# Two turns of a transformer kernel run by token halves

## The reference

```python
h = _rmsnorm(hres, norm_g[i, 0])
m = _diff_attention(...) if i % 2 == 0 else _short_conv(h, w_in[i], conv_w[i // 2], w_out[i])
hres = hres + _rmsnorm(m, norm_g[i, 1])
h = _rmsnorm(hres, norm_g[i, 2])
hres = hres + _rmsnorm(_sqrelu_mlp(h, w_up[i], w_down[i]), norm_g[i, 3])
```

## Time and profile before

| | us |
|---|---|
| median of 3 runs | 1973.28 (1971.84 to 1976.45) |
| the profiled execution's own time | 1971.16 |
| its span, first to last instruction | 1969.4 |
| PE busy | 1887.1 (96%) |
| DVE busy | 1387.8 (70%) |
| ACT busy | 839.2 (43%) |
| POOL busy | 149.8 (8%) |

### The profile page before, as it was taken

How to read it: one execution, slowest core, us unless ns; L and a number is a source line. 1 busy time by engine, 2 the same in 40 slices (tenths; PEclk the granted TensorE clock), 3 DMA queues, 4 the chain that set the end, 5 groups by cost and what they waited for, 6 DMA issues and landing times.

```text
span 1969.4 us, 30367 instructions
## 1 busy us (share of the span) xinstructions
PE 1887.1 (96%) x12322; PEld 1699.5 (86%) x12322; DVE 1387.8 (70%) x2110; ACT 839.2 (43%) x1286; POOL 149.8 (8%) x126
## 2 busy tenths in 40 slices
PE   7999889999999899999998999999899989999996
PEld 6876777899999788989898999999899868988995
DVE  8676738788786866666649877776655469777764
ACT  4555434444443444444435444443422245444441
POOL 3000021000000320000012000000300130000001
PEclk9999999999999999999999999999899989999998
DMA  5220121232333221111111322222122212323221
GB/s 182 67 105 22 54 86 65 86 108 86 108 108 107 86 86 65 44 44 44 65 65 65 108 96 98 89 105 108 45 87 105 86 66 106 107 86 107 107 86 43
DMA packets 26085, 166.54 MB, mean 85 GB/s; under 512 B 3808, under 2 KB 4064, under 8 KB 6624
## 3 DMA queue, kind: packets, MB, share of 16 engines
q1 hardware_dynamic: 25232, 163.52, 23.6%
q10 hardware_dynamic: 720, 1.14, 0.2%
HBM read 162.55 MB, written 2.10 MB: 84 GB/s over the span
## 4 chain that ended last, share of the span: by engine, by line
PE 46%; DVE 4%; ACT 1%; issue 0%; ACTq 0%
PE ps L2857 6%; PE ps L2858 6%; PE ps L2859 6%; PE ps L2873 4%; PE ps L2872 4%; PE ps L2871 4%; PE ps L402 4%; PE ps L404 4%; PE ps L403 4%; DVE ps L560 1%; DVE h L577 1%; DVE z_lo L511 1%; PE ps L2644 0%; PE ps L2646 0%; PE ps L2645 0%; PE ps L449 0%
## 5 line engine op out<-in xcount | busy, mean ns | idle before, releaser
L402 PE MATMUL ps<-z_hi,w_hi 128*128 128x512 f32 (+1 forms) x736 | 259.8, 353 | 31.3 <-DVE z_lo L511 28.0
L384 DVE TENSOR_TENSOR w_lo<-w_raw,w_hi 128x2048 fp32r<-128x2048 f32 x93 | 214.0, 2301 | 64.6 <-ACT w_hi L373 64.5
L403 PE MATMUL ps<-z_lo,w_hi 128*128 128x512 f32 (+1 forms) x736 | 255.3, 347 | 0.0
L404 PE MATMUL ps<-z_hi,w_lo 128*128 128x512 f32 (+1 forms) x736 | 254.8, 346 | 0.0
L2857 PE MATMUL ps<-arena,w_hi 128*128 128x256 f32 (+2 forms) x768 | 245.5, 320 | 0.5 <-DVE acc L2134 0.5
L2858 PE MATMUL ps<-arena,w_hi 128*128 128x256 f32 (+2 forms) x768 | 245.9, 320 | 0.0
L2859 PE MATMUL ps<-arena,w_lo 128*128 128x256 f32 (+2 forms) x768 | 245.4, 320 | 0.0
L373 ACT ACTIVATE w_hi<-w_raw 128x2048 fp32r<-128x2048 f32 x93 | 177.1, 1905 | 71.8 <-PE ps L404 59.0
L402 PEld LDWEIGHTS ps<-z_hi,w_hi 128*128 128x128 f32 x736 | 142.9, 194 | 56.7 <-issue 22.7
L404 PEld LDWEIGHTS ps<-z_hi,w_lo 128*128 128x128 f32 x736 | 142.5, 194 | 17.5
L403 PEld LDWEIGHTS ps<-z_lo,w_hi 128*128 128x128 f32 x736 | 143.1, 194 | 16.8 <-issue 0.7
(11 more groups left out here) (415 smaller groups left out, 5081.8 us busy)
## 6 DMA issues: line engine op xcount, KB each, us to landing
w_raw<-wstream SPq DMA_DIRECT2D x151, 1024.0 KB, 4.8
out<-h SPq DMA_DIRECT2D x8, 256.0 KB, 2.0
w_raw<-wstream SPq DMA_DIRECT2D x2, 512.0 KB, 6.2
h<-xT ACTq DMA_DIRECT2D x4, 256.0 KB, 6.6
h<-xT SPq DMA_DIRECT2D x4, 256.0 KB, 6.1
rope_cs<-pT SPq DMA_DIRECT2D x1, 512.0 KB, 5.5
acc<-pos SPq DMA_DIRECT2D x1, 256.0 KB, 10.5
acc<-lam SPq DMA_DIRECT2D x1, 128.0 KB, 9.9
```

What stands on the lines that cost most here:

```text
L384: dve.tensor_tensor(w_lo[:, slot, :], w_raw[:, slot, :], w_hi[:, slot, :].bitcast(f32), ALU.subtract).then_inc(wlo, 1)
L402: pe.matmul(dst, wh, zh, start=(k == 0), stop=False)
L403: pe.matmul(dst, wh, zl, start=False, stop=False)
L404: last = pe.matmul(dst, wl, zh, start=False, stop=(k == nk - 1))
```

## The change

Both passages (`pi` 3, from the first squared-ReLU stage into the convolution, and `pi` 4, from OUT3 into the second squared-ReLU stage) are written anew as `turn_pe`, `turn_act`, `turn_dve` and `turn_sums`. The last two blocks ahead are run first for tokens 0 to 255 and then for the rest, in tiles of half a bank's width over three banks by turns; the norm behind, z and the squares of the next norm are done for each half; and the first two blocks of the new stage are run for the first half and then for the second. Each half has its own semaphores (`ev`). The product of `scale` goes to `tmp` in SBUF. In PE's queue the column sums and the spread of half 0 stand inside the third half block, those of half 1 inside the first half block of the new stage. DVE's queue interleaves evictions of half 1 and the two new blocks' `dve_lo` with the norm of half 0. With 512 tokens the wide matmul becomes two of 256 columns. The diff, cut:

```diff
+MANY.update({B_MLP2 + down_block(q): 4 for q in (UPS - 2, UPS - 1)})
+MANY.update({B_OUT3 + 2: 2, B_OUT3 + 3: 2})
...
+        def turn_tile(pi, f, hf, t):
+            a, e = part_of(pi, hf)
+            slot = (pair_of(turn_next(pi)) + f) % 2
+            return ps[:, 4 * slot + (turn_tiles(pi) * hf + t) % 3, 0:e - a]
...
+        def turn_square(act, pi, hf, k, pre=0):
+            a, e = in_h(pi, hf)
+            if k >= 2:
+                act.wait_ge(*ev("summed", pi, hf, k - 2, pre))
+            elif not pre and hf == 0:
+                act.wait_ge(summed, summed_to(2 * pi))
+            elif not pre and TURN[pi]:
+                act.wait_ge(s("b_summed"), since("b_summed", 15 * TURN[pi]))
+            if pre:
+                act.wait_ge(*ev("resid", pi, hf, k))
+            else:
+                act.wait_ge(ps_free, tile_count(pi, hf, k))
+            src = h[:, k, a:e] if pre else ac(k)[:, a:e]
+            act.activation(sq[:, k % 2, a:e], src, ACT.Square).then_inc(ev("squared", pi, hf)[0], 1)
+        def turn_zhi(act, pi, hf, k):
+            zi, (a, e), (x, y) = NEXT_Z[pi], in_h(pi, hf), part_of(pi, hf)
+            act.wait_ge(*ev("resid", pi, hf, k))
+            if k == 0 and hf == 0:
+                act.wait_ge(ps_full, turn_base(pi) + 2 * turn_tiles(pi))
+            act.activation(z_hi[:, k, x:y], h[:, k, a:e], ACT.Copy, scale=smc(GAIN[zi][0], GAIN[zi][1] + k)).then_inc(ev("zhi", pi, hf)[0], 1)
...
+        def turn_act(act, pi):
+            g0, late = turn_next(pi), turn_tiles(pi) == 2
+            act_load(act, ACT.Sqrt)
+            for k in range(8):
+                turn_square(act, pi, 0, k)
+            for k in range(4 if late else 1):
+                turn_square(act, pi, 1, k)
+            turn_root(act, pi, 0)
+            if not late:
+                turn_square(act, pi, 1, 1)
+            turn_zhi(act, pi, 0, 0)
+            act_hi(act, g0 % 2, g0 // 2 + 1, turn_base(pi) + 3 * turn_tiles(pi))
+            turn_zhi(act, pi, 0, 1)
+            if late:
+                turn_square(act, pi, 1, 4)
+                turn_zhi(act, pi, 0, 2)
+                turn_square(act, pi, 1, 5)
+                turn_zhi(act, pi, 0, 3)
+                turn_square(act, pi, 1, 6)
+                turn_zhi(act, pi, 0, 4)
+            else:
+                turn_square(act, pi, 1, 2)
+                turn_square(act, pi, 1, 3)
+                turn_zhi(act, pi, 0, 2)
+                turn_square(act, pi, 1, 4)
+                turn_zhi(act, pi, 0, 3)
+                turn_square(act, pi, 1, 5)
+                turn_square(act, pi, 1, 6)
+                turn_zhi(act, pi, 0, 4)
+            turn_square(act, pi, 1, 7)
+            turn_root(act, pi, 1)
+            turn_zhi(act, pi, 0, 5)
+            turn_square(act, pi, 0, 0, 1)
+            turn_square(act, pi, 0, 1, 1)
+            turn_zhi(act, pi, 0, 6)
+            act_next(act, g0 + 1)
+            turn_square(act, pi, 0, 2, 1)
+            turn_square(act, pi, 0, 3, 1)
+            turn_zhi(act, pi, 0, 7)
+            for k in range(4, 8):
+                turn_square(act, pi, 0, k, 1)
+            for k in range(8):
+                turn_zhi(act, pi, 1, k)
+                turn_square(act, pi, 1, k, 1)
+                if k == 3:
+                    turn_pre_root(act, pi, 0)
...
+        def turn_sum(pool, pi, hf, pre):
+            a, e = in_h(pi, hf)
+            for k in range(7 + pre):
+                pool.wait_ge(*ev("squared", pi, hf, k, pre))
+                if k == 0:
+                    if hf == 0:
+                        pool.wait_ge(stat, 2 * pi + 1 + pre)
+                    elif pre:
+                        pool.wait_ge(*ev("stat", pi, 1))
+                    elif TURN[pi]:
+                        pool.wait_ge(s("b_stat"), since("b_stat", 2 * TURN[pi]))
+                    pool.tensor_copy(ssum[:, a:e], sq[:, 0, a:e]).then_inc(ev("summed", pi, hf)[0], 1)
+                else:
+                    pool.wait_ge(*ev("summed", pi, hf, k - 1, pre))
+                    pool.tensor_tensor(ssum[:, a:e], ssum[:, a:e], sq[:, k % 2, a:e], ALU.add).then_inc(ev("summed", pi, hf)[0], 1)
...
+        def turn_prod(pi, hf, k):
+            a, e = part_of(pi, hf)
+            return tt(4 + k % 2, e - a)
+        def turn_scale(dve, pi, hf, k):
+            a, e = in_h(pi, hf)
+            if k == 0:
+                dve.wait_ge(*ev("spread", pi, hf))
+            if k >= 2:
+                dve.wait_ge(*ev("resid", pi, hf, k - 2))
+            elif hf:
+                dve.wait_ge(*ev("resid", pi, 0, 6 + k))
+            dve.scalar_tensor_tensor(turn_prod(pi, hf, k), ac(k)[:, a:e], smc(POST[pi][0], POST[pi][1] + k), turn_roots(pi, hf),
+                                     op0=ALU.mult, op1=ALU.mult).then_inc(ev("scaled", pi, hf)[0], 1)
+        def turn_add(dve, pi, hf, k):
+            a, e = in_h(pi, hf)
+            dve.wait_ge(*ev("scaled", pi, hf, k))
+            dve.tensor_tensor(h[:, k, a:e], h[:, k, a:e], turn_prod(pi, hf, k), ALU.add).then_inc(ev("resid", pi, hf)[0], 1)
+        def turn_zlo(dve, pi, hf, k):
+            zi, (a, e), (x, y) = NEXT_Z[pi], in_h(pi, hf), part_of(pi, hf)
+            dve.wait_ge(*ev("zhi", pi, hf, k))
+            dve.scalar_tensor_tensor(z_lo[:, k, x:y], h[:, k, a:e], smc(GAIN[zi][0], GAIN[zi][1] + k), z_hi[:, k, x:y].bitcast(f32),
+                                     op0=ALU.mult, op1=ALU.subtract).then_inc(ev("zlo", pi, hf)[0], 1)
+        def turn_pre_rcp(dve, pi, hf):
+            a, e = in_h(pi, hf)
+            dve.wait_ge(*ev("rooted", pi, hf, 0, 1))
+            dve.reciprocal(rr[:, 0, a:e], rr[:, 0, a:e]).then_inc(ev("rstd", pi, hf)[0], 1)
+        def turn_dve(dve, pi, evict):
+            g0, late = turn_next(pi), turn_tiles(pi) == 2
+            def add(hf, k):
+                turn_add(dve, pi, hf, k)
+                if k < 7:
+                    turn_scale(dve, pi, hf, k + 1)
+            def lo(hf, k):
+                turn_zlo(dve, pi, hf, k)
+            for n in range(2 * turn_tiles(pi)):
+                evict(0, n)
+            if not late:
+                evict(1, 0)
+            turn_total(dve, pi, 0)
+            evict(1, 0 if late else 1)
+            turn_rcp(dve, pi, 0)
+            if not late:
+                evict(1, 2)
+            turn_scale(dve, pi, 0, 0)
+            add(0, 0)
+            lo(0, 0)
+            evict(1, 1 if late else 3)
+            add(0, 1)
+            dve_lo(dve, g0, g0 % 2)
+            lo(0, 1)
+            add(0, 2)
+            if not late:
+                evict(1, 4)
+                evict(1, 5)
+            lo(0, 2)
+            add(0, 3)
+            evict(1, 2 if late else 6)
+            lo(0, 3)
+            add(0, 4)
+            evict(1, 3 if late else 7)
+            lo(0, 4)
+            add(0, 5)
+            turn_total(dve, pi, 1)
+            lo(0, 5)
+            add(0, 6)
+            turn_rcp(dve, pi, 1)
+            lo(0, 6)
+            add(0, 7)
+            dve_lo(dve, g0 + 1, (g0 + 1) % 2)
+            lo(0, 7)
+            turn_scale(dve, pi, 1, 0)
+            for k in range(8):
+                add(1, k)
+                lo(1, k)
+                if k == 5:
+                    turn_pre_rcp(dve, pi, 0)
...
+        def turn_last_block(pe, pi, f, hf, nk, z, ready, between):
+            b = turn_next(pi) - 2 + f
+            a, e = part_of(pi, hf)
+            nt, base = turn_tiles(pi), turn_base(pi)
+            for t in range(nt):
+                ready(f, hf, t)
+                before = nt * hf + t - 3
+                if before >= 0:
+                    pe.wait_ge(ps_free, base + 2 * nt * (before // nt) + nt * f + before % nt + 1)
+                dst = turn_tile(pi, f, hf, t)
+                for k in range(nk):
+                    if nk * t + k in between:
+                        between[nk * t + k]()
+                    w = (nk * t + k) * P
+                    wh, wl = w_hi[:, b % 2, w:w + P], w_lo[:, b % 2, w:w + P]
+                    zh, zl = z(0, k)[:, a:e], z(1, k)[:, a:e]
+                    pe.matmul(dst, wh, zh, start=(k == 0), stop=False)
+                    pe.matmul(dst, wh, zl, start=False, stop=False)
+                    last = pe.matmul(dst, wl, zh, start=False, stop=(k == nk - 1))
+                last.then_inc(ps_full, 1)
+        def turn_first_block(pe, pi, g, hf, between):
+            b, ntok = turn_next(pi) + g, turn_size(pi)[0]
+            slot = pair_of(b) % 2
+            a, e = part_of(pi, hf)
+            if hf == 0:
+                pe.wait_ge(wlo, b + 1)
+                pe.wait_ge(ps_free, turn_base(pi) + turn_tiles(pi) * (3 + g))
+            for k in range(KD):
+                if g == 0:
+                    pe.wait_ge(*ev("zlo", pi, hf, k))
+                for o in range(2):
+                    if 2 * k + o in between:
+                        between[2 * k + o]()
+                    w = (o * KD + k) * P
```

(59 more changed lines are left out.)

156 lines of the change are left out of this document (143 added, 13 removed).

## The result

The changed kernel takes 1984.04 us (median of 5, 1981.36 to 1988.32) against 1973.08 us of the kernel before beside it (5 runs, 1971.84 to 1976.45): ratio 1.0059, 95% interval 1.0047 to 1.0070, some 11.6 us slower by the ratio and 11.0 by the medians. The forecast was 1982.1 us, 10.9 more than the profiled execution of before.

What follows compares the result with a forecast made beforehand. PE was busy 96% of the span, with DVE setting its waits in both turns. Losses of 2.9 us in turn A and 8.0 in turn B, sum 10.9, on the profiled 1971.16 gave 1982.1 us; range 1972 to 1989.

Steps and rivals of the forecast that it cites:

- What bounds the kernel: DVE sets turn A (second up/down stage into convolution; 17 us lost) and turn B (output into third stage; 15 to 16).
- Half-width durations: Both turns: add or eviction 0.42, scalar-tensor-tensor 0.48, z_hi 0.51, square 0.40, GpSimd's add 0.66 us.
- First half: Turn A from A+0 (block UPS-2 begins): scale 0 at A+18.4, z_lo's first half done at A+40.0; PE's stalls cost nothing.
- Second half: Turn A: z_lo for the second token half takes 17.9 us, last done at A+57.8, against A+49.0 before.
- The port: Both turns: DVE's adds with two SBUF inputs contend with GpSimd; a k takes 1.90 us, without it 1.43.
- Rival 1: Both turns: GpSimd loses the race to DVE's add, running in z_hi's time; 0.3 and 4.9 us lost, 1976.4; chance 0.22.
- Rival 2: Both turns: the port costs nothing at half width; 1.4 us won, 1969.8 us; chance 0.14.
- rival 4: Both turns: GpSimd's half-width add keeps most of its 1.34; up to 29 us lost, 2000; chance 0.05, clock's full price included.
- The end of turn A: Behind the last z_lo DVE needs 8.3 us; convolution block 2 starts at A+66.1 against 63.2: 2.9 lost.
- The end of turn B: From B+0 (OUT3+2 begins): last z_lo at B+55.8, first down block, bound by DVE, at B+79.0 against 71.0: 8.0 lost.
- Bounds without the port: GpSimd's add at 0 port cost: last z_lo at A+51.3 and B+50.1, 3.7 us won in A, 2.3 lost in B.
- A sign that did not come: Both turns: PE waits for z_lo more in total than the earlier 5 us per turn, in pieces of about 1 us.

Runs made afterwards that it cites:

- first trace: The changed kernel's own profiled execution, the slowest of its five runs: 1988.32 us.
- psum_product: Changed kernel with the residual addition's product in a PSUM bank in place of SBUF, half 1's column sums moved to another bank: 1975.28 us, ratio 1.0015.
- quiet_pool: Changed kernel, product still in SBUF, GpSimd adding only two columns of the squares for the next norm (results not the reference's): 1971.28 us, ratio 1.0003.
- second trace: The changed kernel without further edit, traced once more: 1981.82 us.

## Why the prediction was right

- *What bounds the kernel.* Right. DVE sets both turns, and the gain of a faster first half is capped by it.
- *Half-width durations.* Add 0.42, scale 0.47 to 0.49, z_lo 0.49, z_hi 0.51, square 0.40: as taken from the earlier trace rows. GpSimd's add at 258 columns, for which I took 0.66 (bounds 0.67 and 1.34), is 0.74.
- *First half.* Scale 0 came 0.9 sooner than forecast in A and 0.7 in B, half 0 of z_lo within 1.0 us. The stall at the tile is 2.8 (about 2 forecast), the one at the column sums 2.1 and 3.3 (about 2). "Nothing of that reaches the end" was wrong: the column sums hold the root and z_hi 5, and DVE waits too. In the first trace PE ran at 0.69 in 1395 to 1405 in place of 0.84, DVE stood 1.62 us for the column sums in place of 0.79, and half 0 and the last z_lo came 0.8 us later (A+40.6 and A+58.6).
- *Second half.* Forecast 17.9 in A, measured 18.1 (1410.31 to 1428.45). The step is 1.96 where I had 1.90, the wait for z_hi 0 is 1.99 where I had 1.8.
- *The port.* Right in mechanism and in size. In half 1 five of the eight adds of turn A cost 0.55 more, 2.7 us where I had 2.85. Of the other three one (at 1410.81) meets only the end of a GpSimd add and takes 0.45, one (1414.05) begins ahead of GpSimd's, and one stands behind the reciprocal, beside which GpSimd's add runs in full. Moving the product to PSUM takes 3.0 us off half 1 in A (18.1 to 15.1) and 3.3 in B. In half 0 of A four adds and two z_lo run longer than elsewhere, by 1.8 and 0.95 us, 2.8 together where I had 2.6; the same move takes 1.3 off that half (A+39.7 to A+38.4), since the long z_lo stay. The price of the port in the prediction, 12.3 us (1982.1 against 1969.8), is more than the product's place, 8.7: z_lo meets GpSimd in either kernel, and the bound is too low (below). Rival 1, the lost race: in front of the five long adds of half 1 GpSimd asks 0.05 to 0.06 ahead of DVE and gets in; at 1414.05 DVE is first, once, and GpSimd is the one that waits. Rival 2 fell, by `psum_product` and `quiet_pool`, rival 4 by the 0.74.
- *The end of turn A.* Missed by 1.0 in the second trace and 2.5 in the first. The failing step is "block 0 is complete 0.8 behind z_lo 7": w_hi started 1.8 behind it (1430.26 against 1428.45), since the last matmuls of block 0 ran at a granted clock of 0.56 in that stretch. I had put the clock into the range only; in the first trace the last z_lo was 0.8 late as well and half block 1 ran at 0.50 too, and PE, not DVE, was last there.
- *The end of turn B.* Forecast 8.0, measured 7.1 and 7.8, with DVE full to the low parts.
- *Bounds without the port.* Turn A was put 1.3 to 1.7 us too early against `quiet_pool`, turn B within 0.6. The bound takes 6.5 us off the last z_lo of A, but the sum charges the port 2.6 and 2.85 only: 1.05 of it has no term. Without that it is A+52.4, beside the A+52.6 of `quiet_pool` and the A+53.5 of `psum_product`, in which z_lo still loses 1.1 us to GpSimd. `quiet_pool` is near it by a trade, though: it keeps long adds in half 0 and saves 1.4 us at z_hi 0.
- *A sign that did not come.* I expected PE to wait for z_lo longer in total, in pieces of about 1 us. It waits 3.2 and 5.6 us, 8.8 in all against 9.8 before, in pieces of up to 2.0; the loss shows in the waits for the tile, the sums and the low parts.
- "No DMA is added and none waits": held in the second trace but for the 0.6 us above; the first has the odd load.

The forecast of 1982.1 and the second trace's 1981.8 agree partly by cancelling: A lost 0.9 more and B 0.9 less than forecast. It also starts from one execution of before, 1.9 us under the median beside the change; from median to median the kernel lost 11.0 us, forecast were 10.9.
